# Experts: the next pass's tokens are picked inside a pass, and twelve weight places turn slot by slot

## The reference

```python
def hier_moe(x, w_group, b_group, w_expert, b_expert, w_gate_up, w_down):
...
    grp = jnp.argmax(g_logits, axis=-1)
...
    top_v, top_i = lax.top_k(e_in_grp, TOP_K)
    weights = (jax.nn.softmax(top_v, axis=-1) * p_grp).reshape(n_asg)
    expert = (grp[:, None] * EXPERTS_PER_GROUP + top_i).reshape(n_asg)
...
    def expert_block(args):
        xb, e = args
        gate, up = jnp.split(xb @ w_gate_up[e], 2, axis=-1)
        return (jax.nn.silu(gate) * up) @ w_down[e]
...
    y = jnp.zeros((n_tok, D), x.dtype).at[tok_s].add(y_buf[dest] * w_s[:, None].astype(x.dtype))
```

## Time and profile before

| | us |
|---|---|
| three runs | 1661.64, 1663.04, 1663.22 |
| their median | 1663.04 |
| span of the profiled execution, first to last instruction | 1661.7 |
| PE, DVE, ACT, POOL busy in it | 1534.3, 1005.3, 679.3, 361.5 |

### The profile page before, as it was taken

One profiled execution on the slowest core, in us unless ns is written; L12 is line 12 of the kernel. 1 busy time (PEld: TensorE's weight loads), 2 busy tenths in 40 slices (PEclk: granted clock), 3 DMA queues, 4 the chain that ended last, 5 costly groups with the idle time before them and its releaser, 6 DMA issues.

```text
span 1661.7 us, 30547 instructions
## 1 busy us (share of the span) xinstructions
PE 1534.3 (92%) x12376; PEld 1275.5 (77%) x12377; DVE 1005.3 (60%) x1756; ACT 679.3 (41%) x986; POOL 361.5 (22%) x223
## 2 busy tenths in 40 slices
PE   9999987777777767999999999999999999999998
PEld 8889974444444334788889998888888899988887
DVE  5875732222221222888758678866788658788854
ACT  6464421111111001555535755544454436655542
POOL 1120040000000000154203614430344107324410
PEclk9999998898988888999999999999999999999999
DMA  8545699999999999654545465445554545465450
GB/s 350 199 173 208 242 374 430 431 431 434 432 432 433 434 431 428 244 189 172 179 160 179 157 224 189 174 176 208 191 189 167 179 157 197 153 218 191 168 184 26
DMA packets 37284, 421.05 MB, mean 253 GB/s; under 512 B 4330, under 2 KB 6522, under 8 KB 9154
## 3 DMA queue, kind: packets, MB, share of 16 engines
q1 hardware_dynamic: 36514, 415.49, 64.5%
q0 software_dynamic: 672, 4.15, 0.6%
HBM read 416.45 MB, written 3.18 MB: 253 GB/s over the span
## 4 chain that ended last, share of the span: by engine, by line
PE 82%; DMA 11%; DVE 3%; issue 2%; ACT 1%; ACTq 1%; SPq 0%; DVEq 0%
PE bank L1276 19%; PE bank L1293 10%; PE bank L1278 10%; DMA ring<-moe_w_dram 8%; PE bank L785 7%; PE bank L787 6%; PE bank L786 6%; PE bank L1164 6%; PE bank L1295 5%; PE bank L1193 3%; DMA area<-moe_w_dram 2%; PE bank L1099 2%; DVE sq L2523 1%; DMA ring<-first_w_dram 1%; PE bank L1376 1%
## 5 line engine op out<-in xcount | busy, mean ns | idle before, releaser
L1276 PE MATMUL bank<-h_split,w_hi 128*128 128x512 f32 x1408 | 489.7, 392 | 0.6 <-DVE h_split L2109 0.6
L1276 PEld LDWEIGHTS bank<-h_split,w_hi 128*128 128x128 f32 x1408 | 264.3, 188 | 59.6 <-DVE h_split L2109 1.2
L1761 ACT CAST w_hi<-ring 128x2048 fp32r<-128x2048 f32 (+2 forms) x124 | 232.8, 1879 | 146.0 <-PE bank L1295 102.7
L680 POOL TENSOR_TENSOR area<-area,stat 128x256 f32<-128x256 f32 x88 | 215.3, 2447 | 293.9 <-DVE area L2600 293.9
L1278 PE MATMUL bank<-h_split,lo_last 128*128 128x256 f32 x840 | 234.8, 280 | 0.0
L2118 DVE TENSOR_TENSOR lo_last<-ring,w_hi 128x2048 fp32r<-128x2048 f32 (+3 forms) x75 | 174.2, 2325 | 7.2 <-ACT w_hi L1761 7.1
L1278 PE MATMUL bank<-h_split,lo_first 128*128 128x256 f32 x568 | 158.8, 280 | 0.0
L1278 PEld LDWEIGHTS bank<-h_split,lo_last 128*128 128x128 f32 x840 | 157.7, 188 | 0.0
L1164 PE MATMUL bank<-ring,sq 128*32 128x256 f32 x1408 | 112.5, 484 | 43.1 <-DVE sq L2523 33.1
L1164 PEld LDWEIGHTS bank<-ring,sq 128*32 128x32 f32 x1408 | 63.6, 137 | 86.0 <-issue 75.4
L2118 DVE TENSOR_TENSOR lo_first<-ring,w_hi 128x2048 fp32r<-128x2048 f32 (+3 forms) x50 | 116.8, 2335 | 2.8 <-ACT w_hi L1761 2.8
(11 more groups left out here) (482 smaller groups left out, 3457.7 us busy)
## 6 DMA issues: line engine op xcount, KB each, us to landing
ring<-moe_w_dram SPq DMA_DIRECT2D x38, 3072.0 KB, 32.4
ring<-layer_w_dram SPq DMA_DIRECT2D x56, 1536.0 KB, 6.7
area<-moe_w_dram SPq DMA_DIRECT2D x18, 3072.0 KB, 31.7
ring<-layer_w_dram SPq DMA_DIRECT2D x32, 1408.0 KB, 6.4
ring<-layer_w_dram SPq DMA_DIRECT2D x34, 1024.0 KB, 5.2
ring<-first_w_dram SPq DMA_DIRECT2D x21, 1536.0 KB, 6.9
ring<-moe_w_dram SPq DMA_DIRECT2D x12, 1536.0 KB, 12.5
area<-moe_w_dram SPq DMA_DIRECT2D x4, 1536.0 KB, 10.0
```

The lines of the kernel that those rows point to most:

```text
L680: pool.tensor_tensor(up, up, stat[:, 3, :], ALU.mult).then_inc(S("up_scaled"), 1)
L1276: pe.matmul(halves(first_bank + side), hi_of(q)[:, cols], h_split[:, :, k, :], start=k == 0, stop=False, skip_group_check=True)
L1761: act.copy(hi_of(q)[:, cols], ring[:, PLACES[q % len(PLACES)], cols]).then_inc(S("hi_a_ready"), 1)
```

## The change

- **Places turn slot by slot.** `TURNING` lists the twelve places, and slot s of all experts' slots takes the next one. Each refill is one slot (1.5 MiB, rows of 12,288 bytes) that waits only for the use of the slot that held its place. `moe_w` is laid out slot by slot. Every place has a semaphore of its own; places that the second block's ring also uses share its semaphore. The very last slot comes in three DMAs of one down chunk each. The last expert now lies in `area`, so the fifth slot of the second block no longer waits for `moe_done`.
- **Tokens are picked a pass ahead.** In pass n PE picks the tokens of pass n + 1 after gate and up, and turns them before down; the hidden block is turned before `combine`. ACT and DVE follow that order. The pick of pass 1 stands before the loop, and the last pass picks once more for a pass that does not come.
- **A table of passes.** DVE has to know which expert pass n + 1 belongs to. Three more small products on PE, one comparison on DVE and one copy on ACT make `plan`, two rows of 49 integers, before the loop; DVE and ACT then run one loop over all passes, and DVE reads four numbers of `plan` in each.
- **Layout.** The table of constants `expert` (32 columns) becomes `count` (49 columns), so `consts` has 17 columns more and what lies behind it moves: `ring` begins at byte 22,080 of each partition where it began at 22,016 (which is 86 x 256), and `area` at 172,160 where it began at 171,680. `h_t` moves behind `probs`. Some semaphores are merged under one name.

```diff
-MOE_RING = (0, 1, 6, 7, 2, 3, 4, 5)
-EXPERT_SETS = 3
+AREA_PLACES = range(RING, RING + EXPERT_SLOTS)
+TURNING = (0, 1, 3, 6, *AREA_PLACES, 4, 2, 5, 7)
+FIRST_PLACES = TURNING
+MOE_PLACES = len(FIRST_PLACES)
+EXPERT_SETS = len(TURNING) // EXPERT_SLOTS
+LOOP_AT = 4
...
+def moe_place(s):
+    return FIRST_PLACES[s] if s < MOE_PLACES else TURNING[(s - MOE_PLACES) % len(TURNING)]
+def moe_before(s):
+    return s - len(TURNING)
...
         def _(sp):
-            def fill(m):
-                half = slice(m % 2 * SLOT, (m % 2 + 1) * SLOT)
-                sp.dma_start(moe_slot(m), moe_w[m // 2][:, half]).then_inc(pair_full[m // 2], 16)
+            def fill(s):
+                place = moe_place(s)
+                sp.dma_start(moe_slot(place), moe_w[s]).then_inc(moe_full[place], 16)
...
-            for m, n in ((0, 18), (1, 19), (5, 19), (2, 20), (6, 20), (4, 21), (7, 21)):
+            for s, n in ((0, 18), (1, 19), (2, 19), (3, 20), (8, 20), (9, 21), (10, 21)):
...
-            def refill(done, held, source, pairs=EXPERT_PAIRS):
-                before = passes_until(done)
-                for i in range(pairs):
-                    sp.wait_ge(S(EXPERT_SLOT_USED[2 * i + 1]), before)
-                    pair = EXPERT_PAIRS * held + i
-                    sp.dma_start(moe_pair(pair), source(i)).then_inc(pair_full[pair], 16)
-                return before
...
+            def refill(slots, done, source):
+                for s in slots:
+                    of, i = divmod(moe_before(s), EXPERT_SLOTS)
+                    if s == slots[0] or i == 0:
+                        before = passes_until(done(of))
+                    sp.wait_ge(S(EXPERT_SLOT_USED[i]), before)
+                    place = moe_place(s)
+                    if s < MOE_SLOTS - 1:
+                        sp.dma_start(moe_slot(place), source(s)).then_inc(moe_full[place], 16)
+                        continue
+                    for (landed, _), at in zip(last_parts, range(0, SLOT, D)):
+                        sp.dma_start(moe_slot(place)[:, at:at + D], source(s)[:, at:at + D]).then_inc(landed, 16)
...
                 at = q % len(PLACES)
-                if q == len(PLACES) - 1:
-                    sp.wait_ge(S("moe_done"), 1)
-                elif q >= len(PLACES):
+                if q >= len(PLACES):
                     slot_consumed(sp, q - len(PLACES))
...
+            def expert_weights(e, at, turn):
+                s = EXPERT_SLOTS * e + at // SLOT
+                place = moe_place(s)
+                if s == MOE_SLOTS - 1:
+                    landed, times = last_parts[at % SLOT // D]
+                    pe.wait_ge(landed, 16 * times)
+                elif at % SLOT < D:
+                    pe.wait_ge(moe_full[place], 16 * (landed_before[place] + moe_fills(s)) + 16 * turn)
+                    settled(pe)
+                return moe_slot(place)[:, at % SLOT:at % SLOT + D]
...
-                pe.wait_ge(S("share_t_ready"), nth)
...
+                pe.wait_ge(S("share_t_ready"), nth)
+                pick_tokens(nth + 1)
+
+                pe.wait_ge(S("hid_ready"), nth)
+                settled(pe)
+                pe.transpose(ps[1][:, 0:P], two["hid"], ident).then_inc(S("hid_turned"), 1)
 
                 pe.wait_ge(S("y_ready"), nth)
                 settled(pe)
                 combine(False)
                 pe.wait_ge(S("share_ready"), nth)
+                pe.wait_ge(S("picked_ready"), nth + 1)
...
                 pe.wait_ge(S("hid_t_ready"), nth)
                 settled(pe)
+                turn_tokens()
...
+            dve.wait_ge(S("planned"), 5)
+            selected(*planned(1))
+            dve.wait_ge(S("shares_made"), 1)
+            shared(0, 0)
+            hidden(1)
+            picked_moved(2)
...
+            with dve.Fori(1, total_passes(packed)) as n:
+                selected(*planned(n + 1))
+                shared(*planned(n))
+                hidden(n + 1)
+                picked_moved(n + 2)
```

More of the change, by code:

```diff
@@ L490, in program, with total_passes, moe_slot @@
         layer_full = [S(f"layer_full{i}") for i in range(len(PLACES))]
[L491 to L503, removed]
+        own_landed = [S(f"own_landed{i}") for i in range(3)]
+        third_landed = layer_full[0], layer_full[4], own_landed[0]
+        moe_full = {place: layer_full[PLACES.index(place)] if place in PLACES else S(f"moe_full{place}")
+                    for place in TURNING}
+        landed_before = {place: FIRST_FULL[PLACES.index(place)] if place in PLACES else 0 for place in FIRST_PLACES}
+        last_parts = (own_landed[0], 2), (own_landed[1], 1), (own_landed[2], 1)
+        def total_passes(packed):
+            return nc.s_assert_within(packed // 16 + packed % 16, EXPERTS, PASSES,
+                                      skip_runtime_bounds_check_because="T tokens have TOP_K experts each")
+        def moe_slot(place):
+            at = (place - RING) * SLOT
+            return ring[:, place, :] if place < RING else area[:, at:at + SLOT]
         diff_stat = ffs[:, 3, 0, :]
@@ L568, in _ @@
[L568 to L575, removed]
@@ L1119, in _, with pick_tokens @@
             pe.matmul(ps[0][0:1, 352:352 + EXPERTS], passes_of[:, 0:1], strict[0:EXPERTS, 0:EXPERTS],
[L1120 to L1134, removed]
-                pe.wait_ge(S("share_t_ready"), nth)
+                      start=True, stop=True).then_inc(S("planned"), 1)
+            pe.matmul(ps[3][0:EXPERTS, 400:401], const("tri", EXPERTS)[:, 0:EXPERTS], passes_of[:, 0:1],
+                      start=True, stop=True).then_inc(S("planned"), 1)
+            def pick_tokens(nth):
                 pe.wait_ge(S("select_ready"), nth)
@@ L2493, in _ @@
             for choice, where in enumerate((e1, e2)):
-                own.mark(tt(where, over(const("expert"), TT), over(best_at[:, :, choice], EXPERTS, 2), ALU.is_equal))
+                own.mark(tt(where, over(const("count")[:, 0:EXPERTS], TT), over(best_at[:, :, choice], EXPERTS, 2), ALU.is_equal))
             own.wait()
@@ L2568, in _, with planned @@
-            with dve.Fori(1, EXPERTS) as e:
-                expert(e)
+            dve.wait_ge(S("tables_moved"), 16)
+            selected(0, 0)
+            dve.wait_ge(S("planned"), 2)
+            ts(ended, const("count", EXPERTS), ps[3][0:EXPERTS, 400:401], None, ALU.is_ge).then_inc(S("planned"), 1)
+            picked_moved(1)
+            def planned(n):
+                e = dve.value_load(plan[0:1, bass.ds(n, 1)], min_val=0, max_val=EXPERTS - 1)
+                before = dve.value_load(plan[0:1, bass.ds(n + PASSES + 1, 1)], min_val=0, max_val=PASSES)
+                first = nc.s_assert_within((n - before) * P, 0, (WINDOWS - 1) * P,
+                                           skip_runtime_bounds_check_because="an expert has at most T tokens")
+                return e, first
@@ L2916, in layouts @@
         down = i["w_down"][0, e].reshape(4, P, D).transpose(1, 0, 2)
-        both = flat(up, down).reshape(P, EXPERT_PAIRS, 2 * SLOT)
-        moe_w[EXPERT_PAIRS * e:EXPERT_PAIRS * (e + 1)] = both.transpose(1, 0, 2)
+        both = flat(up, down).reshape(P, EXPERT_SLOTS, SLOT)
+        moe_w[EXPERT_SLOTS * e:EXPERT_SLOTS * (e + 1)] = both.transpose(1, 0, 2)
     layer_w = np.empty((LAYERS * LAYER_SLOTS, P, SLOT), np.float32)
```

180 lines of the change are left out of this document (78 added, 102 removed).

## The result

The changed kernel takes 1674.78 us (median of four runs, 1673.51 to 1675.52) against 1663.13 for the kernel before (median of four runs too); the ratio is 1.0066, 95% interval 1.0052 to 1.008. It is slower by some 11.6 us where +3.7 was forecast, and 1674.78 lies outside the range. The profiled execution took 1673.51, with a span 10.0 us longer than before.

The account below looks back on a forecast made before the run. The experts' DMA stream was taken as the bound: 256.3 + 111 x 3.67 = 663.7, plus 7.2 gives 670.9 against 667.2. That +3.7 on a span of 1661.7 gives 1665.4, plus 1.3 for the median 1666.7 us; range 1660.5 to 1673.

Parts of the forecast that it names:

- Bound and waits: Expert passes: the DMA stream sets the pace, so taking 93.6 us of DVE and ACT waits from PE gains nothing.
- The hole: Stream start, 237.5 to 256.3 us: 4.3 us lost there stay lost; bounds -4.3 and +1, chance of closing 9%.
- The table: Table of passes before the expert loop: +0.1 us, from below 0 to +1, not counted in the sum.
- Single slots at 3.67: Expert stream: 111 slots that come alone take 3.67 us each against 3.635 for half a pair; bounds 3.635 and 3.74.
- the shift: Addresses off a 256-byte multiple: 0.07 us a slot, charged only on the third of the slots that lie in `area`.
- dearer in `area`: Sign that the forecast is right: singles land 3.65 to 3.70 us apart, and dearer in `area`.
- Charging the price per row: Expert stream: the extra 0.09 us of an `area` pair goes by rows, and a single has as many as a pair.
- The second figure, 3.675: Expert stream: with two 32-byte beats in `ring` and four in `area`, 3.675 us a slot, adding 0.6 us to the sum.
- the shift is paid by every row: Rival for the expert stream: 3.70 to 3.74 us a slot, end +7 to +11.4, say 1671 us; chance 20%.
- The end: From slot 126's landing to the last down's end: PE's fixed chain, 7.2 us taken, between 6.3 and 8.5.
- the allowance for a lower clock: PE's chain after slot 126: about 2.2 us longer if its first three groups run at the lower clock; 7.2 taken.
- The moved tiles I count at 0; no row prices them: Tiles moved to other addresses: cost taken as 0, with no bound given.

Follow-up runs that it names:

- Kernel 8: Changed kernel's pick ahead with the old pair transfers, old order of places, `ring` and `area` at their old places: 1662.36 us, 0.9994 of the kernel before.
- kernel 9: Changed kernel, single slots kept, with `ring` and `area` at multiples of 256 bytes and `h_split` 32 bytes further on: 1662.45 us, 0.9994 of the kernel before.
- kernels 7: Changed kernel's pick ahead with old pairs and order, `ring` and `area` at multiples of 256 bytes, `h_split` 32 bytes on: 1659.32 us, 0.9977 of the kernel before.
- kernel 5: Kernel before with 96 unused bytes ahead of `area`, which then starts at a multiple of 256 bytes: 1674.45 us, 1.0066 of the kernel before.
- kernel 10: Changed kernel with `h_split` (and `hid_own` behind it) moved by 96 bytes inside `area`: 1668.39 us, 1.0026 of the kernel before.
- kernels 1: Kernel before with 17 unused columns of constants, so every tile behind them lies 64 bytes further: 1665.95 us, 1.0014 of the kernel before.
- kernel 12: Kernel before with 32 unused columns of constants, so everything behind them lies 128 bytes further: 1664.86 us, 1.0009 of the kernel before.
- kernels 3: Changed kernel with every tile back at its old place within 256 bytes, single slots kept: 1664.82 us, 1.0006 of the kernel before.

## Why the prediction was wrong, point by point

- **Bound and waits: right.** The rate stayed flat, PE's waits turned into waits for slots, and 93.6 us of them were worth nothing. Kernel 8 shows the same with the stream unchanged.
- **The hole: right.** Slot 15 lands between 254.5 and 257.5 in all sixteen profiles, in both orders.
- **The table: +0.1, right as far as it shows.** The first gate-up product came 2.4 us later (236.76 for 234.37), which looked like its price. Over all runs it starts at 233.4 to 237.2 with the old first stage and at 234.0 to 236.8 with the new one: that is scatter.
- **Single slots at 3.67: too low, the first step that failed.** 3.690 was measured: 110 x 0.02 = 2.2 us, and a lone step 0.6. Over the 3.635 of half a pair the sum had 0.015 for a single and 0.07 / 3 = 0.023 for the shift; the runs show 0.020 (kernel 9 against 7) and 0.035 (the changed kernel against 9). The shift was left on `area`'s third of the slots, although front and bounds said that `ring` loses its multiple of 256 bytes; all twelve places paid, and the sign "dearer in `area`" did not come. The reading behind it was wrong too: `area`'s later landings before cost the stream nothing, since kernel 5 aligns `area` and keeps the mean of 3.635. That shifted addresses then did cost something is luck as far as it rests on those pairs. Charging the price per row was right: 4 ns a row of either length. The second figure, 3.675 by the Trainium skill's beats, does not follow from the 0.07 that the first one uses: five beats for 0.07 are 0.014 each, (8 x 2 + 4 x 4) / 12 = 2.67 beats a slot are 0.037, and with 3.65 that is 3.687 and not 3.675. The rival "the shift is paid by every row" came nearest in mechanism; its 3.70 to 3.74 us a slot were a little dear, and it too counted nothing for the moved tiles, below.
- **The end: 6.1 for 7.2, a little under its low bound of 6.3.** The turn took 0.22 us where 0.42 was counted, and the granted clock was 1.00 although PE had waited for each slot, so the allowance for a lower clock was not used. 6.0 or 6.1 us in most kernels with the pick ahead, 7.7 in kernel 10, where the granted clock was 0.50 as the last slots came.
- **"The moved tiles I count at 0; no row prices them": the step that failed outright.** They cost 3.9 us, and the prediction gave them no bound. "No row prices them" was true, and for that reason it should have been a range. Kernel 10 gives them back with 96 bytes: 993.6 us for 998.4 from the last down to the end. What the runs do not show is why PE pays.
- **The sum.** Forecast +3.7 on the last down; measured +6.1, that is 3.9 for the addresses of the transfers (111 x 0.035), 2.2 for singles, 0.6 for the lone step, 0.7 for the hole, and -1.2 for a shorter end than the 7.3 us that the kernel before took after its slot 126. With 3.9 from the second block the span grew by 10.0. The remaining 1.7 of the 11.6 is that the median of the four runs stands 3.1 us over the profiled span, where it was 1.4 before: the profiled execution was the fastest of the four.

## What to carry to other kernels

A table that grows by 17 columns moves every tile behind it: look at the addresses of a changed program before its schedule. The large transfers here were cheapest with `ring` at a multiple of 256 bytes (1% a slot), and the distance between a matmul's moving tile and its weights went with 1 to 2% of the matmul, with no wait to be seen; compare a group's mean ns of one, and move one tile by some tens of bytes to see if it is that. Work taken off an engine that waits for a stream only lengthens its waits; transfers of half the size paid a little each. Landings that come later in some places are not yet a cost: compare the mean over a whole round of places.

## What the runs showed of the hardware that was not expected

- The same matmuls, with the same shapes and full clock, at 348.1 to 354.7 ns a pair by tens of bytes of distance between tiles. In kernel 5 the second block grew by 13.1 us, 9.2 of them in gate and up.
- A single transfer of 1.5 MiB costs 0.020 us more than half of one of 3 MiB in a full queue (kernels 7 and 9), and 0.035 more again if neither `ring` nor `area` starts at a multiple of 256 bytes; half a pair pays 0.017 for that (kernels 1, 12). Both are 4 ns a row. `area` 160 bytes past a multiple costs nothing while `ring` stands at one (kernels 3 and 9, the kernel before and 5).
- Each kernel with single transfers has one lone step in its stream, 0.3 to 1.5 us over the others, that is never made up; with pairs a late landing (7.54, kernel 12) was followed by an early one (7.15). In the changed kernel it comes at 301.9, soon after a packet of program code that took 1.07 us. That this is the cause is not shown: five other such packets between 264 and 350 us, of 1.02 to 1.09 us each, have no such step behind them.
